# Constant TensorE products around the parameter transposes of a two-block transformer kernel

## The chip, the cores and the metric

One NeuronCore of a Trainium2 chip runs the whole program. The metric is the time of one execution on the device in microseconds (us), and the median over runs is compared. Times of single instructions below come from one profiled execution of the same program.

## What is computed

The reference runs two blocks over 256 tokens of width 1024 in float32. The first block has two layers, each a mixer and an expert stage:

```
for l in range(DEPTH):                      # DEPTH = 2
    mod = silu(c) @ ada_w[l] + ada_b[l]     # shifts, scales and gates
    xm = rms_norm(x, norm_mix_w[l]) * (1 + sc1) + sh1
    proj = xm @ w_in[l]                     # queries, keys, values, pool, gates
    x = x + g1 * ((sigmoid(ga)*attention + sigmoid(gp)*pool) @ w_out[l])
    xf = rms_norm(x, norm_ffn_w[l]) * (1 + sc2) + sh2
    x = x + g2 * peer_ffn(xf)               # top 16 of 16384 experts, 8 heads
x = rms_norm(x, final_norm_w)
for i in range(4):                          # differential, MoBA, window, differential
    x = x + mixer_i(rms_norm_2(x, attn_norm_g[i]))
    x = x + sqrelu_mlp(rms_norm_2(x, mlp_norm_g[i]))
```

`peer_ffn` gathers, for each token and head, 16 rows of `expert_u` and 16 rows of `expert_v` from HBM. The output is the last norm of x.

## The kernel before, in words

The tokens are two tiles of 128 rows and stay in SBUF (`x_res`). Each engine has its own program, and all waits are semaphores written out by hand. The two layers of the first block are one hardware loop on every engine (`Fori(0, DEPTH)`); the four layers of the second block are unrolled.

A weight unit is 1024 x 512. ScalarE rounds a quarter of it to the float32r type (L1367 in the first block, L1491 in the second), VectorE or GpSimd subtracts to get the rest (L1835, L1691, L2407), and TensorE makes three float32r products for one float32 product (`three`, L770, L771, L772). Each is 128x512 wide. Attention, the out projections (L740), the transposes (L706) and the expert products use plain float32.

At the start of a layer of the first block the order is as follows. SyncE loads five small parameter vectors into `prow` (L547 to L551). TensorE waits for them (`s_par`), transposes `prow` into PSUM bank `psT` 0 (L889) and raises `p_tr`. VectorE waits for `p_tr`, sets the same memory to ones (L1919), copies the transposed parameters to `pcol` (L1920), forms shift and scale (L1893 to L1895), waits for ScalarE's sums of squares (L1305), and takes the row statistics (L1629, L1630). ScalarE takes the square root (L1307), VectorE scales the rows (`xn`, L1635), TensorE transposes them in four groups of four (L706), VectorE and ScalarE make the high and low parts of the transposed rows (L1843, L1373, L1853), and TensorE starts the first in-projection (L770). In layer 0 TensorE reaches this point after the last of four column sums of the modulation matrix (`mix_sum`, L865); in layer 1 after the `go` of `layer_end`, with which SyncE lets all engines pass once it has cleared the semaphores (L643).

A gather end is the end of an expert stage: the last expert rows land in `vbuf`, `ring` and `pr`, TensorE multiplies them (L1059), VectorE adds the result to x (L2219, L2220), and the layer ends. There are two, near 1021 us and 1999 us of the profiled execution. After the second, the last four layers begin: TensorE transposes their parameter rows `rows2` (L1105), waits for `p_col`, then for x to be normed (L1638), transposes two groups of it (L706), and starts the first in-projection when ScalarE (L1491, then L1515) and VectorE (L1691, L1740) have made its parts. SyncE's queue loads the lambda vectors and weights there (L655, L666).

PSUM tile `psS` has two banks of 512 floats. Bank 1 is used later in each layer by gate rows, scores and query products.

Of the kernel before, what the change touches and what calls it, by code (L numbers as in the profile page):

```python
# [35 lines left out]
UC = 512  # L36
# [181 lines left out]
def program(nc, T, out):  # L218
    with ExitStack() as ctx:
# [10 lines left out]
        def cst(name):  # L230
            lo, hi = COFF[name]
            return const[:, lo:hi]

        ident = cst("ident")
# [48 lines left out]
        psS = ctx.enter_context(nc.psum_tensor("psS", [P, 2, 512], F32))  # L283
# [234 lines left out]
        def _(sp):  # L518
# [127 lines left out]

            C = Counts(RING2)
            C.slot[0] = -1
            for i, m in enumerate(MIXERS2):
# [10 lines left out]
                def unit2(src, kc=KC, cols=UC):  # L660
                    slot, _ = C.next_slot()
                    if C.unit > RING2:

                        sp.wait_ge(lo_ready, NPC * (C.unit - RING2))
                    dst = ring[:, slot, :, :].rearrange("p k n -> p (k n)")[:, 0:kc * cols]
                    sp.dma_start(dst.rearrange("p (k n) -> p k n", k=kc), src).then_inc(ld[slot], 16)  # L666

                for n, (lo, cols) in enumerate(units):
                    if i == 0 and n == 0:
                        C.next_slot()  # L670
                        continue
# [28 lines left out]
        def _(pe):  # L700
# [13 lines left out]
            def norm(C):  # L714
                C.norm += 1
                C.xn += 2
                pe.wait_ge(xn_ready, C.xn)
                tr_all(C, xn)
# [150 lines left out]
            def ada_sum(n):  # L869
# [10 lines left out]
                                       start=True, stop=True)  # L880
                mm.then_inc(s_ada, 1)

            pe.wait_ge(s_const, 32)
            for n in range(NMIX):
                mix_sum(n, first=True)
            with pe.Fori(0, DEPTH) as l:
                C = Counts()
                pe.wait_ge(s_par, 80)
                pe.transpose(psT[:, 0, 0:76], prow[0:76, :], ident[0:76, 0:76]).then_inc(p_tr, 1)  # L889
                C.tr = 0  # L890
                norm(C)

# [9 lines left out]
                for n in range(8):  # L902
                    first_linear(C, n, sums_in(n))
                    if n == 4:
                        pe.wait_ge(gate_read, 1)
                        pe.wait_ge(lin_used, 4)
                        for g in range(NPG):
                            for kt in range(NT):
# [3 lines left out]
                                               start=(kt == 0), stop=(kt == NT - 1))  # L912
                        mm.then_inc(pl_mm, 1)
                    if n == 5:
                        pe.wait_ge(pl_cp, 1)
                        pe.wait_ge(s_wide, 80)
                        for g in range(NPG):
                            mm = pe.matmul(psT[:, g // 2, (g % 2) * S:(g % 2 + 1) * S], mixw[:, g, :], mT[:, g, :],
                                           start=True, stop=True)
# [183 lines left out]
            C.slot[0] = -1  # L1103
            pe.wait_ge(s_rows, 96)
            pe.transpose(psT[:, 0, 0:80], rows2[0:80, :], ident[0:80, 0:80]).then_inc(p_tr, 1)  # L1105
            pe.wait_ge(p_col, 1)

            def row_groups(C, first, used=None):
# [174 lines left out]
        def _(act):  # L1283
# [236 lines left out]
            for i, m in enumerate(MIXERS2):  # L1520
                if m is DIFF:
                    act.wait_ge(lam_x, 3 * (i // 3) + 1)
                    act.activation(st[:, 8:10], st[:, 6:8], ACT.Exp).then_inc(lam_x, 1)
                n_in, widths = (4, [2 * cols for _, cols in SWA_UNITS]) if m is SWA else (6, [D] * 6)
                high_with_xT(C, pcol[:, 8 * i:8 * i + 8], w=widths[0])
                row_squares(C)
# [954 lines left out]
```

## Time and profile before

| what | value |
|---|---|
| median of 3 runs | 3300.11 us (3299.2 to 3303.0) |
| span of the profiled execution | 3298.6 us |
| TensorE busy | 2344.9 us (71%) |
| VectorE busy | 2128.5 us (65%) |
| ScalarE busy | 936.9 us (28%) |
| GpSimd busy | 1009.8 us (31%) |
| mean granted TensorE clock | 0.832 |

### The profile page before, as it was taken

What the parts mean: (1) busy time and instruction counts of PE and PEld (TensorE: products, weight loads), DVE (VectorE), ACT (ScalarE), POOL (GpSimd) and SP (SyncE); (2) the same over time, 40 slices, a digit from 0 to 9 for tenths busy, and PEclk for the clock granted to TensorE, in tenths of its full rate; (3) what the DMA queues carried; (4) which work ended last, traced back from release to release, by engine and by line L of the source; (5) the groups of instructions that cost most, each with busy time, mean ns of one, the idle gap of its engine ahead of it and who ended that gap; (6) DMA issues with size and microseconds to landing.
All of it is one profiled execution on the core that took longest, in us unless ns stands there. A gap on an engine that the chain in (4) does not pass through costs nothing.

```text
span 3298.6 us, 35236 instructions
## 1 busy us (share of the span) xinstructions
PE 2344.9 (71%) x12383; PEld 1724.4 (52%) x12383; DVE 2128.5 (65%) x4436; ACT 936.9 (28%) x1486; POOL 1009.8 (31%) x1044
## 2 busy tenths in 40 slices
PE   4997444454336996544444337899999999999898
PEld 3855222222004854222222005699879978987797
DVE  6965876677757865776677755565655555555654
ACT  2411111011003501111111004454555444445443
POOL 0201766767771102766667760000000000000000
PEclk9998667777667997666777668799999987999899
DMA  8764999999998754999999994245525532553353
GB/s 316 280 226 140 406 407 407 408 406 409 405 405 306 268 211 174 407 407 407 407 409 409 400 407 180 77 173 185 182 99 179 182 111 103 185 187 140 103 192 126
DMA packets 311815, 892.92 MB, mean 271 GB/s; under 512 B 22424, under 2 KB 31616, under 8 KB 311552
## 3 DMA queue, kind: packets, MB, share of 16 engines
q0 software_dynamic: 147456, 536.94, 41.0%
q1 hardware_dynamic: 164224, 354.32, 30.1%
q8 instruction: 68, 1.11, 0.1%
q14 instruction: 67, 0.55, 0.0%
HBM read 890.13 MB, written 1.05 MB: 270 GB/s over the span
## 4 chain that ended last, share of the span: by engine, by line
PE 46%; DMA 15%; POOL 13%; issue 13%; DVE 11%; ACT 1%; SPq 0%; DVEq 0%; POOLq 0%; ACTq 0%; PEld 0%
DMA proj<-in_expert_u,eidx 13%; PE lin L770 8%; PE lin L771 8%; PE lin L772 8%; POOL proj L2423 7%; POOL vbuf L2436 3%; PE lin L740 3%; POOL ring L2436 3%; PE psS L821 2%; DVE proj L2130 2%; PE psT L772 2%; PE psT L771 2%; PE psS L771 2%; PE psS L772 2%; PE psT L770 2%
## 5 line engine op out<-in xcount | busy, mean ns | idle before, releaser
L2130 DVE CUSTOM_DVE_ANT_0 proj<-proj,psT 128x1024 f32<-128x1024 f32 x512 | 615.2, 1219 | 360.1 <-DMA proj<-in_expert_u,eidx 339.2
L1691 DVE TENSOR_TENSOR weights_split<-ring,weights_split 128x1024 fp32r<-128x1024 f32 (+1 forms) x376 | 450.5, 1207 | 376.3 <-ACT weights_split L1491 373.8
L2423 POOL DMA_INDIRECT proj<-in_expert_u,eidx x512 | 485.0, 947 | 573.8 <-DVEq L2104 318.0
L1491 ACT ACTIVATE weights_split<-ring 128x1024 fp32r<-128x1024 f32 (+1 forms) x376 | 391.5, 1046 | 467.7 <-PE lin L772 291.6
L1046 PE MATMUL psS<-const,pT 128*128 128x16 f32 x64 | 18.8, 373 | 430.6 <-DVE pT L2117 392.8
L1059 PE MATMUL lin<-ring,rowb 128*32 128x512 f32 x896 | 171.1, 802 | 207.1 <-DMA pr<-in_expert_v,pT 138.2
L770 PE MATMUL lin<-weights_split,xT_high 128*128 128x512 f32 (+1 forms) x736 | 297.2, 404 | 11.3 <-DVE xT_low L1740 5.2
L772 PE MATMUL lin<-weights_split,xT_high 128*128 128x512 f32 (+1 forms) x736 | 288.9, 393 | 0.0
L1059 PE MATMUL lin<-vbuf,rowb 128*32 128x512 f32 x1024 | 183.1, 867 | 130.9 <-DVE rowb L2157 130.9
L1434 ACT ACTIVATE gel<-hdot 128x16 f32<-128x16 f32 x32 | 6.9, 216 | 934.2 <-DVE hdot L2130 934.2
L2436 POOL DMA_INDIRECT vbuf<-in_expert_v,pT x256 | 240.1, 938 | 78.1 <-issue 77.5
L1046 PEld LDWEIGHTS psS<-const,pT 128*128 128x128 f32 x64 | 16.0, 311 | 471.0 <-DVE pT L2142 379.6
L1015 PE MATMUL psS<-xT,ring 128*128 128x256 f32 x1024 | 244.9, 400 | 3.1 <-ACT pT L1415 3.1
L1015 PEld LDWEIGHTS psS<-xT,ring 128*128 128x128 f32 x1024 | 203.4, 202 | 62.6 <-issue 33.5
L2436 POOL DMA_INDIRECT ring<-in_expert_v,pT x224 | 210.2, 938 | 68.3 <-issue 66.5
L770 PE MATMUL lin<-weights_split,act_split 128*128 128x512 f32 x512 | 200.1, 391 | 0.0
L771 PE MATMUL lin<-weights_split,act_split 128*128 128x512 f32 x512 | 199.5, 390 | 0.0
L772 PE MATMUL lin<-weights_split,act_split 128*128 128x512 f32 x512 | 199.2, 389 | 0.0
L1059 PEld LDWEIGHTS lin<-ring,rowb 128*32 128x32 f32 x896 | 32.6, 130 | 306.3 <-DMA pr<-in_expert_v,pT 165.9
L771 PE MATMUL lin<-weights_split,xT_low 128*128 128x512 f32 (+1 forms) x480 | 187.3, 390 | 0.0
L770 PEld LDWEIGHTS lin<-weights_split,xT_high 128*128 128x128 f32 x736 | 143.3, 195 | 46.1 <-issue 10.4
L1059 PEld LDWEIGHTS lin<-vbuf,rowb 128*32 128x32 f32 x1024 | 39.2, 147 | 235.8 <-issue 233.6
(279 smaller groups left out, 5008.2 us busy)
## 6 DMA issues: line engine op xcount, KB each, us to landing
ring<-in_mlp_w_up SPq DMA_DIRECT2D x32, 2048.0 KB, 8.7
ring<-in_mlp_w_down SPq DMA_DIRECT2D x32, 2048.0 KB, 7.7
ring<-in_w_in SPq DMA_DIRECT2D x16, 2048.0 KB, 10.0
ring<-in_w_query SPq DMA_DIRECT2D x16, 2048.0 KB, 18.3
vbuf<-in_ada_w SPq DMA_DIRECT2D x12, 2048.0 KB, 12.0
ring<-in_diff_w_in SPq DMA_DIRECT2D x12, 2048.0 KB, 8.1
ring<-in_ada_w SPq DMA_DIRECT2D x8, 2048.0 KB, 12.5
ring<-in_moba_w_in SPq DMA_DIRECT2D x6, 2048.0 KB, 7.9
```

The lines of the kernel that those rows point to most:

```text
L740: mm = pe.matmul(lin[:, pair + t, :], lhs[:, k, t * P:(t + 1) * P], rhs[:, k, :], start=(k == 0), stop=(k == kc - 1))
L770: pe.matmul(out_ap, lhs[0], rhs[0], start=first, stop=False, skip_group_check=True)
L771: pe.matmul(out_ap, lhs[1], rhs[0], start=False, stop=False, skip_group_check=True)
L772: return pe.matmul(out_ap, lhs[0], rhs[1], start=False, stop=last, skip_group_check=True)
L821: mm = pe.matmul(psS[:, g % 2, t * S:t * S + n], qkT[lo:hi, qb, t * P:(t + 1) * P], qkT[lo:hi, kb, 0:n], start=True, stop=True)
L1015: mm = pe.matmul(psS[:, 1, (b % 2) * S:(b % 2 + 1) * S], ring[:, j, k, b * P:(b + 1) * P], xT[:, k, :], start=(k == 0), stop=(k == KC - 1))
L1059: mm = pe.matmul(lin[32 * b:32 * b + 32, 2 * half + t, :], wst[:, cb % 2, 4 * b + s, :], vrow(SETROWS * s + b)[:, half * 512:(half + 1) * ...
L1491: act.activation(part(p, 0, kind, w), raw_piece(slot, p, kind, w), ACT.Copy).then_inc(hi_ready, 1)
L1691: dve.tensor_tensor(part(p, 1, kind, w), raw_piece(slot, p, kind, w), part(p, 0, kind, w).bitcast(F32), ALU.subtract).then_inc(lo_ready, 1)
L2130: dve.tensor_tensor_reduce(ubuf[:, n % GB, :], ubuf[:, n % GB, :], x_row, 1.0, 0.0, ALU.mult, ALU.add, hdot[:, cb, k:k + 1]).then_inc(h_re ...
L2423: pool.indirect_dma_start(out=ubuf[:, (16 * cb + k) % GB, :], out_offset=None, in_=table["u"], in_offset=bass.IndirectOffsetOnAxis(ap=eidx ...
L2436: pool.indirect_dma_start(out=vrow(SETROWS * s + b), out_offset=None, in_=table["v"], in_offset=bass.IndirectOffsetOnAxis(ap=eidxT[:, cb % ...
```

## The change

In the TensorE program a function `keep_clock(n)` issues n float32 products. The stationary operand is the 128x128 identity, the moving one the first 512 columns of the constant pool table, and the result goes to `psS` bank 1. Nothing reads it, they wait for nothing, and they signal nothing. Both operands are loaded at the program's start (`s_const`, waited for ahead of the loop).

- Ahead of the wait for `s_par` and the transpose L889: 6 products, in layer 0 and in layer 1.
- Behind that transpose: 3 products, in both layers.
- Behind the transpose L1105, ahead of the wait for `p_col`: 7 products, once.

```diff
+            def keep_clock(n):
+
+                for _ in range(n):
+                    pe.matmul(psS[:, 1, :], ident, cst("pool")[:, 0:UC], start=True, stop=True, skip_group_check=True)
+
             pe.wait_ge(s_const, 32)
             for n in range(NMIX):
                 mix_sum(n, first=True)
             with pe.Fori(0, DEPTH) as l:
                 C = Counts()
+                keep_clock(6)
                 pe.wait_ge(s_par, 80)
                 pe.transpose(psT[:, 0, 0:76], prow[0:76, :], ident[0:76, 0:76]).then_inc(p_tr, 1)
+                keep_clock(3)
                 C.tr = 0
                 norm(C)
...
             pe.wait_ge(s_rows, 96)
             pe.transpose(psT[:, 0, 0:80], rows2[0:80, :], ident[0:80, 0:80]).then_inc(p_tr, 1)
+            keep_clock(7)
             pe.wait_ge(p_col, 1)
```

## Rows read from the trace of the kernel before

**Rows 1.** The page: span, busy time of each engine, engines of the chain that ended last.

```profile
span 3298.6 us, 35236 instructions
...
PE 2344.9 (71%) x12383; PEld 1724.4 (52%) x12383; DVE 2128.5 (65%) x4436; ACT 936.9 (28%) x1486; POOL 1009.8 (31%) x1044
...
PE 46%; DMA 15%; POOL 13%; issue 13%; DVE 11%; ACT 1%; SPq 0%; DVEq 0%; POOLq 0%; ACTq 0%; PEld 0%
```

**Rows 2.** The chain that ended last, in time order, layer 0's first half: start, us, what.

```profile
54.58 1.13 PE psT L706 x4
...
59.99 0.76 PE lin L770
...
63.31 0.29 PE lin L771
64.06 0.23 PE lin L771
...
192.86 12.02 PE lin L740 x28
```

**Rows 3.** The timeline around layer 0's parameter transpose.

```profile
47.48 1.87 PE L865 MATMUL psS<-const,rope_t 128*128 128x1 f32 x8 [4.04 <-DVE rope_t L1861]
...
49.21 0.37 PE L889 MATMUL psT<-const,prow 76*128 76x76 f32 x1
...
50.07 0.17 DVE L1919 MEMSET prow<- 128x128 f32 x1 [0.45 <-DVE modc L1913]
...
52.41 0.17 DVE L1629 TENSOR_SCALAR st<-st 128x2 f32<-128x2 f32 x1 [1.28 <-ACT tokb L1305]
```

**Rows 4.** The timeline around layer 1's parameter transpose.

```profile
1019.14 1.08 PE L1059 MATMUL lin<-ring,rowb 128*32 128x512 f32 x3
...
1019.99 1.08 PE L1059 MATMUL lin<-ring,rowb 128*32 128x512 f32 x3
...
1022.54 0.35 SPq L547 DMA_DIRECT2D prow<-in_ada_b  x1
...
1026.65 0.39 PE L889 MATMUL psT<-const,prow 76*128 76x76 f32 x1 [5.56 <-DMA prow<-in_pool_scale]
...
1027.26 0.17 DVE L1919 MEMSET prow<- 128x128 f32 x1 [3.26 <-remote]
...
1028.35 0.17 DVE L1629 TENSOR_SCALAR st<-st 128x2 f32<-128x2 f32 x1
```

**Rows 5.** The timeline at the start of the last four layers.

```profile
1999.91 0.28 PE L1105 MATMUL psT<-const,wrow 80*128 80x80 f32 x1 [0.98 <-SPq L643]
...
2007.15 1.94 PE L706 MATMUL psT<-const,x_res 128*128 128x128 f32 x8 [6.96 <-DVEq L2248]
...
2009.91 1.54 ACT L1515 ACTIVATE xT_high<-psT,pcol 128x256 fp32r<-128x256 f32 x4
...
2012.36 0.79 PE L770 MATMUL lin<-weights_split,xT_high 128*128 128x512 f32 x1 [3.27 <-DVE xT_low L1740]
```

**Rows 6.** TensorE by stretch: us, busy us (instructions), granted clock, DMA share, GB/s.

```profile
1030.00:1036.00 6.00, 4.26 (x17) 0.50 0.95 311
...
1990.00:1990.50 0.50, 0.14 (x4) 1.00 0.08 33
1995.00:1995.50 0.50, 0.07 (x4) 0.76 0.00 0
...
2015.50:2016.00 0.50, 0.50 (x3) 0.76 0.00 0
...
2138.50:2139.00 0.50, 0.50 (x4) 0.88 0.00 0
```

**Rows 7.** The timeline after the first attention of the last four layers.

```profile
2133.92 0.80 PE L770 MATMUL lin<-weights_split,xT_high 128*128 128x512 f32 x1 [0.99 <-DVE xT_low L1740]
```

**Rows 8.** TensorE by stretch again, two attention stretches of the last four layers.

```profile
2094.50:2124.50 30.00, 27.93 (x90) 0.50 0.00 1
...
2410.00:2440.00 30.00, 30.00 (x189) 1.00 0.00 1
```

## The prediction

> **What bounds the kernel now.** I read the page first. The span is 3298.6 us; the median of the runs is 3300.11, so 1.5 us lie around it. TensorE is busy 71% of it, VectorE 65%, and 46% of the chain that ended last is TensorE's [rows 1]. No engine bounds it all: the change must be read at its three places.
>
> The chain in time order shows what counts there. In layer 0 it goes from the last column sum over ScalarE's squares and the norm to TensorE's transposes at 54.58, then over VectorE and ScalarE to the first in-projection at 59.99 [rows 2]. Its products stand 0.43 us apart until 63.3 and 0.23 us from then on: they began at half clock and went to full. At the last four layers it is alike: products begin at 2012.36 and the granted clock changes between 2015.5 and 2016.0 [rows 5, 6]. About 3.4 us, or 8 products, run at half clock, and layer 1 has the same code. Saving that is worth 8 x (0.43 - 0.23) = 1.6 us a place.
>
> The timeline then shows what TensorE could be late for. In layer 0 the parameter transpose follows the column sums with no wait; `prow` has long landed [rows 3]. In layer 1 it waits 5.56 us for it, until 1026.65, and in the last part TensorE idles 6.96 us between its parameter transpose and the next ones [rows 4, 5].
>
> **The price of one product.** The 128x512 float32 products of the out projection take 12.02 us for 28, 0.43 us each at full clock [rows 2]. At half clock the expert products, 128x512 float32 too, start 0.85 us apart (1019.14, 1019.99) [rows 4]. So 6 products cost 5.1 us at half clock; if the clock rises after 3.4 us of them, 4 are slow and 2 fast: 4 x 0.85 + 2 x 0.43 = 4.3 us. The first in-projections rose after 3.3 to 3.4 us [rows 2, 5, 6], so I take 4.3. The upper end is 5.1: after the first attention products began at 2133.92 and the clock rose only between 2138.5 and 2139.0 [rows 6, 7].
>
> **Six ahead, layer 0.** Nothing hides them. TensorE ends its column sums at 49.35 and has the transpose ready to go, so the transpose is 4.3 us late (upper 5.1). VectorE waits for it at L1919, and everything of VectorE's is queued behind. But its statistics at 52.41 had waited 1.28 us for ScalarE [rows 3], and ScalarE's squares wait for nothing that is late. So the layer is 4.3 - 1.3 = 3.0 us late (upper 3.8). SyncE's queue is not delayed; its weights have landed or are on their way, and later loads wait for pieces of VectorE and TensorE that are late too, so nothing takes the delay back. Lower end: 0, if some transfer behind it ends the waits anyway.
>
> **Six ahead, layer 1.** SyncE issues the first load behind the `go` at 1022.54, so TensorE starts its products at about 1022.7 and ends at 1027.0 (upper 1027.8). The load they cover ends its wait at 1026.65 [rows 4]. The transpose is 0.3 us late (upper 1.2), and here VectorE has no slack: it waited for the transpose, and its statistics followed its own work at 1028.35 without a wait [rows 4]. So +0.3.
>
> **Three behind.** 1.3 us at full clock, 2.6 at half. In layer 0 5.0 us lie between the end of the parameter transpose (49.21 + 0.37) and the row transposes at 54.58 [rows 2, 3], 3.7 once its slack of 1.3 is used up; in layer 1 the steps between are the same. They are covered and cost nothing. Without this cover they would cost their 1.3 us.
>
> **Seven ahead of the last four layers.** 3.0 us at full clock, 6.0 at half. `p_tr` is raised ahead of them, so VectorE's copy isn't late; TensorE's wait for `p_col` is met meanwhile. They end at 2003.2 to 2006.2, and the next transposes start at 2007.15 [rows 5]. Cost 0. If x were normed earlier by over 0.9 us, the slow case would begin to cost.
>
> **What the clock gives back.** After the three products TensorE idles 3.7 - 1.3 = 2.4 us to the row transposes. The record has an idle of 3.1 us that the full clock outlived (products again at 1990.4, clock 1.00) and another of 3.1 us that it did not (1995.4, clock 0.76 in that half us) [rows 6]. So at 2.4 us I take full clock for the first transposes. Four of these take 1.13 us from their wake to their end at half clock [rows 2], and half of that is pace: 0.5 us saved a layer, 1.0 in all. Bounds: 0, if the six did not raise the clock, and 0.5.
>
> From there to the first in-projection are 5.4 us (54.58 to 59.99) in which TensorE only transposes and waits for VectorE. At full clock it would be busy for about 2 of them. At half clock the stretch from 1030 to 1036 had it busy 4.26 of 6 us, and the clock did not rise [rows 6]. That sort of work is thin; I take it that the clock falls before or soon after the in-projection begins, and that its 3.4 slow us stay. Bounds: 0 and 1.6 us for each layer. At the last four layers, 4.3 us without any product lie between the transposes (over at about 2008.1) and 2012.36, and those first transposes wait to be read until 2009.91 by ScalarE's own queue [rows 5]. Earlier transposes bring nothing, and the idle is longer than the 3.1 us that ended full clock. I take 0; bounds 0 and 1.6.
>
> The Trainium skill, in "TensorE: Matmul & The Clock Gate", Part 4: PE-mode transpose, says that transposes do not count as TensorE activity in the way of products. The row of 1030 to 1036 agrees so far. By it the in-projections' slow start stays in every case, and the sum is the one below; without it, it would be up to 3.2 us lower, as in the first rival.
>
> **The sum.** 3.0 + 0.3 - 1.0 = +2.3 us against the profiled execution, 3298.6 to 3300.9, and with the 1.5 us around it 3302.4. That is 0.07%. A measurement of this kernel can tell about 0.2% (6.6 us) from no change: so, within it.
>
> **Rivals.**
> - *The clock holds through to the in-projections.* Then 1.6 us go at each of three places: 2.3 - 4.8 = -2.5, 3297.6. For it: an idle of 3.1 us once did no harm, and the transposes may count. Against: the thin 5.4 us, and the 4.3 us of nothing in the last case. Also within 0.2%. Chance 0.12.
> - *The products are just in the way.* The six never raise the clock while they last, as after the first attention, where 4.7 us of work went by first; no transposes are faster; and the in-projections, shifted, also wait 4.7 us for the clock instead of 3.4, 0.6 us more at each of three. 3.8 + 1.2 + 1.8 = +6.8, 3306.9. It decides once the rise comes over 4.3 us after the products begin. This is also how the change would fail to do what it says. For it: one such case among three rises read [rows 6, 7]. Chance 0.14, half of it over 0.2%.
> - *A long stretch changes its clock (slower).* In the last four layers two attentions hold quite different states: 30 us at half clock with TensorE busy 27.93, and 30 us at full clock with it busy all the time [rows 8]. A busy engine thus does not always win its clock back. If the shift of some us made the one at 2410 fall and stay, it would cost 15 to 30 us: 3317 to 3332. It decides if TensorE's work thins out for a moment there. Against: the three runs lie within 3.8 us of each other, so such a flip seems rare. Chance 0.08.
> - *The same, faster.* One of the slow attentions keeps full clock and gives up to 14 of its 28 busy us; I take 10: 3292. Same evidence against. Chance 0.06.
>
> **How the numbers follow.** The forecast has 0.60, for 3302.4. Faster by over 0.2% is the last rival, 0.06, and one in a hundred for luck: 0.07. Slower by over 0.2% is half of the second and the third: 0.15. The rest, 0.78, is no change. The range takes in the first two rivals with their ends, 3297 to 3308; the two clock flips are left out, 0.14.
>
> **What would show it.** In the changed kernel's timeline: in layer 0 six products from 49.35, four of them 0.85 us apart, and the parameter transpose near 53.6; VectorE's statistics 3 us later than 52.41, and no wait for ScalarE ahead of them. In layer 1 the transpose near 1027 us plus layer 0's shift. Row transposes at the pace of full clock in both layers. In the last part seven products 0.43 us apart, over before the transposes. All three first in-projections with about 8 products 0.43 us apart: if they start 0.23 apart, I was wrong about the thin stretch. If the layer starts less late than the transpose minus 1.3 us, the delay found slack that I did not see. A changed clock in an attention stretch would overrule all of it.

## The result and the profile after

| | before | after |
|---|---|---|
| median | 3298.77 us (20 runs, 3286.67 to 3303.04) | 3307.60 us (20 runs, 3290.86 to 3312.26) |
| span of the profiled execution | 3298.6 us | 3305.8 us |

The ratio on record is 1.0033, 95% interval 1.0022 to 1.0045: slower by 0.33%, past the 0.2% that I took for the limit of a measurement. The medians alone lie 8.8 us (0.27%) apart. The median lies inside my range at its upper edge, but the forecast was "no change". The runs of both kernels fall into two groups, which the three runs that I had did not show: 3 of 20 of before lie at 3286.7 to 3287.6 and the other 17 have a median of 3299.8; of after, 3 lie at 3290.9 to 3297.7 and the other 17 have a median of 3309.3. The profiled pair below differs by 7.2 us, a little less than the medians do.

The page after. TensorE is busy 16.4 us more than before and the span is 7.2 us longer [rows 1]:

```profile
span 3305.8 us, 35336 instructions
...
PE 2361.3 (71%) x12433; PEld 1727.3 (52%) x12433; DVE 2128.1 (64%) x4436; ACT 936.6 (28%) x1486; POOL 1006.6 (30%) x1044
...
PE 47%; DMA 15%; POOL 13%; issue 12%; DVE 10%; ACT 1%; SPq 1%; POOLq 0%; DVEq 0%; PEld 0%; ACTq 0%
```

The instructions of the added line (count, shortest, median and longest ns, first and last start, forms), in the changed kernel:

```profile
L886 PE MATMUL psS<-const x50: 592/592/1201, 49.2 to 2013.0; 128*128 128x512 f32 x50
```

The code issues 9 + 9 + 7 = 25 products. The profile counts **50 matmul instructions: a plain float32 product of 128x128x512 is two**. The trace of before had said so too. The same view of its out projection:

```profile
L740 PE MATMUL lin<-ring,xT x256: 592/592/676, 186.6 to 1238.1; 128*128 128x512 f32 x128
...
L740 PE MATMUL lin<-vbuf,xn x64: 592/592/595, 216.8 to 1208.9; 128*128 128x512 f32 x64
```

These are 320 instructions for 160 products in the code (two layers of 4 x 8 x 2 + 2 x 4 x 2). The 0.43 us that I took as the price of a product [rows 2] is that of half a product.

The timeline of the changed kernel in layer 0, which answers to [rows 2, 3] (start, us, what, and in brackets the idle time before and what ended it):

```profile
49.17 7.54 PE L886 MATMUL psS<-const 128*128 128x512 f32 x12
...
56.55 0.23 PE L895 MATMUL psT<-const,prow 76*128 76x76 f32 x1
56.62 2.78 PE L886 MATMUL psS<-const 128*128 128x512 f32 x6
56.88 0.17 DVE L1927 MEMSET prow<- 128x128 f32 x1 [7.28 <-PE psT L895]
...
57.96 0.17 DVE L1637 TENSOR_SCALAR st<-st 128x2 f32<-128x2 f32 x1
...
60.13 1.09 PE L706 MATMUL psT<-const,xn 128*128 128x128 f32 x8 [0.73 <-DVE xn L1643]
...
65.54 0.47 PE L770 MATMUL lin<-weights_split,xT_high 128*128 128x512 f32 x1 [1.56 <-DVE first_xT_low L1861]
65.85 0.40 PE L771 MATMUL lin<-weights_split,first_xT_low 128*128 128x512 f32 x1
66.08 0.40 PE L772 MATMUL lin<-weights_split,xT_high 128*128 128x512 f32 x1
```

The six products take 7.5 us. VectorE waits 7.28 us for the transpose behind them, and no longer waits for ScalarE. The products of the first in-projection now start 0.23 us apart: "warm" in what follows, and "cold" where they start 0.43 us apart, at half clock.

Layer 1 in the changed kernel, which answers to [rows 4]:

```profile
1022.42 0.61 PE L1066 MATMUL lin<-ring,rowb 128*32 128x512 f32 x3
...
1029.00 7.43 PE L886 MATMUL psS<-const 128*128 128x512 f32 x12 [5.97 <-issue]
1036.27 0.23 PE L895 MATMUL psT<-const,prow 76*128 76x76 f32 x1
...
1045.25 0.47 PE L770 MATMUL lin<-weights_split,xT_high 128*128 128x512 f32 x1 [1.56 <-DVE first_xT_low L1861]
1045.56 0.39 PE L771 MATMUL lin<-weights_split,first_xT_low 128*128 128x512 f32 x1
```

SyncE's first load starts at 1025.43. TensorE's products, which wait for nothing, start only 3.57 us behind it; I had them 0.2 us behind it. The transpose comes 10.84 us behind the load, 4.11 before.

The last four layers, which answer to [rows 5]:

```profile
2007.39 6.21 PE L886 MATMUL psS<-const 128*128 128x512 f32 x14
2014.51 1.06 PE L706 MATMUL psT<-const,x_res 128*128 128x128 f32 x8 [0.91 <-DVEq L2256]
2019.72 0.80 PE L770 MATMUL lin<-weights_split,xT_high 128*128 128x512 f32 x1 [4.14 <-DVE xT_low L1748]
2020.31 0.63 PE L771 MATMUL lin<-weights_split,xT_low 128*128 128x512 f32 x1
```

The seven products end 0.9 us ahead of the next transposes: covered, with little to spare. From the parameter transpose to the first in-projection it is 12.45 us in both kernels.

TensorE by stretch in the changed kernel (us, busy us (instructions), granted clock, DMA share, GB/s), which answers to [rows 6]:

```profile
1030.00:1040.00 10.00, 9.27 (x20) 0.84 1.00 346
1040.00:1046.00 6.00, 3.00 (x19) 1.00 1.04 388
...
2019.50:2023.00 3.50, 3.28 (x8) 0.51 0.17 66
```

Where the 7.2 us arise, from starts of the same instructions in both profiled executions (after minus before, cumulative):

| place | us |
|---|---|
| parameter transpose, layer 0 | +7.34 |
| first in-projection | +5.55 |
| first out projection | +4.42 |
| first gather of expert rows | +3.44 |
| SyncE's first load of layer 1 | +2.89 |
| parameter transpose, layer 1 | +9.62 |
| first in-projection | +9.32 |
| first out projection | +8.03 |
| first gather of expert rows | +7.03 |
| parameter transpose, last layers | +7.36 |
| end | +7.21 |

### The profile page after: what moved, and what is told of

Read it like the earlier page. It is cut to its first block, busy times and chain, and to the rows that moved or that the text cites. A ratio compares the mean times of both kernels' runs of the same rounds, so it can differ in the third digit from the quotient of the medians.

```text
span 3305.8 us, 35336 instructions
## 1 busy us (share of the span) xinstructions
PE 2361.3 (71%) x12433; PEld 1727.3 (52%) x12433; DVE 2128.1 (64%) x4436; ACT 936.6 (28%) x1486; POOL 1006.6 (30%) x1044
## 4 chain that ended last, share of the span: by engine, by line
PE 47%; DMA 15%; POOL 13%; issue 12%; DVE 10%; ACT 1%; SPq 1%; POOLq 0%; DVEq 0%; PEld 0%; ACTq 0%
DMA proj<-in_expert_u,eidx 13%; PE lin L770 8%; PE lin L771 8%; PE lin L772 8%; POOL proj L2431 7%; POOL vbuf L2444 4%; PE lin L740 3%; POOL ring L2444 3%; PE psS L821 2%; PE psT L772 2%; PE psT L771 2%; PE psS L771 2%; PE psS L772 2%; PE psT L770 2%; PE psS L770 2%
## 5 line engine op out<-in xcount | busy, mean ns | idle before, releaser
L1499 ACT ACTIVATE weights_split<-ring 128x1024 fp32r<-128x1024 f32 (+1 forms) x376 | 391.5, 1046 | 467.7 <-PE lin L772 291.5
L1022 PE MATMUL psS<-xT,ring 128*128 128x256 f32 x1024 | 246.1, 401 | 3.1 <-ACT pT L1423 3.1
L770 PEld LDWEIGHTS lin<-weights_split,xT_high 128*128 128x128 f32 x736 | 142.7, 194 | 49.4 <-issue 11.5
## 6 DMA issues: line engine op xcount, KB each, us to landing
vbuf<-in_ada_w SPq DMA_DIRECT2D x12, 2048.0 KB, 11.9
```

The lines of the kernel that those rows point to most:

```text
L770: pe.matmul(out_ap, lhs[0], rhs[0], start=first, stop=False, skip_group_check=True)
L1022: mm = pe.matmul(psS[:, 1, (b % 2) * S:(b % 2 + 1) * S], ring[:, j, k, b * P:(b + 1) * P], xT[:, k, :], start=(k == 0), stop=(k == KC - 1))
L1499: act.activation(part(p, 0, kind, w), raw_piece(slot, p, kind, w), ACT.Copy).then_inc(hi_ready, 1)
```

## The experiments

In runs 1 to 4 the gathers take as long as in the first profile. In runs 5 to 14 each of the two gathers takes 57 to 72 us longer, and the kernel before, run beside them, is over 110 us slower too; there its totals spread over some 35 us, so I compare each run with before beside it, and mechanisms by stretches between starts. The record numbers the chip 6 for runs 1 to 4 and again for 13 and 14, 3 for runs 5 to 8 and 5 for 9 to 12: whether the chip makes the difference is not shown. "Attention" below is that of the last four layers. The three sites are called six, three and seven. In the expectations, the relu is ScalarE's first activation behind an attention.

**1. Only the three behind the transpose.**

```diff
                 pe.transpose(psT[:, 0, 0:76], prow[0:76, :], ident[0:76, 0:76]).then_inc(p_tr, 1)
+                keep_clock(3)
```

> Only the three products behind the parameter transposes stay. Theory A (a float32 product of 128x128x512 is two matmul instructions, and the six ahead of the transpose are the whole loss): in layer 0 the three run as six instructions from 49.6 to 54.0 or 54.7, against row transposes at 54.58 before, so they cost 0 to 0.2 us; the clock rises during them, the first in-projection starts 0.23 us apart, and layer 0 and layer 1 each gain 1 to 2 us: 2 to 4 us faster than before. Rival B (only the long run of all nine raises the clock, three cannot): parameter transposes on time, first in-projection at 0.43 us a product as before, 0 to +0.5 us.

3299.05 us against 3299.85, ratio 1.0002 (0.9987 to 1.0016). The timeline of this kernel:

```profile
49.05 4.39 PE L886 MATMUL psS<-const 128*128 128x512 f32 x6
54.26 1.10 PE L706 MATMUL psT<-const,xn 128*128 128x128 f32 x8 [0.81 <-DVE xn L1641]
...
59.66 0.77 PE L770 MATMUL lin<-weights_split,xT_high 128*128 128x512 f32 x1 [1.55 <-DVE first_xT_low L1859]
60.23 0.63 PE L771 MATMUL lin<-weights_split,first_xT_low 128*128 128x512 f32 x1
60.65 0.63 PE L772 MATMUL lin<-weights_split,xT_high 128*128 128x512 f32 x1
```

Three products, six instructions, take 4.39 us, nearly what I had forecast for six products, and the row transposes are not late: covered. But the in-projections start 0.43 us apart again. These products run in cover and buy nothing.

**2. Only the six ahead.**

```diff
+                keep_clock(6)
                 pe.wait_ge(s_par, 80)
```

> Only the six ahead of the parameter transposes stay. Theory A: twelve instructions, parameter transpose 7.3 us late in layer 0 (5.5 us late on VectorE) and some 6.5 us more in layer 1. Without the three behind, TensorE idles 3.5 us ahead of the row transposes, the clock falls, and less is given back: +8 to +12 us. Rival B (the three behind do nothing): the same as the whole change, +7 us, with the in-projections at full clock from their start.

3311.16 us, ratio 1.0045 (1.0028 to 1.0062); the profiled span is 11.5 us longer than before's. The whole loss comes with the six. It is larger than the change's 7.2 us: in layer 0 the in-projection began cold here, and the first gather came 7.5 us late, where the change had 3.4.

**3. Only the seven ahead of the last layers.**

```diff
             pe.transpose(psT[:, 0, 0:80], rows2[0:80, :], ident[0:80, 0:80]).then_inc(p_tr, 1)
+            keep_clock(7)
```

> Only the seven ahead of the last four layers stay. Theory A: they fill an idle of TensorE, over before 2007.15, and the first in-projection starts at 2012.36 at half clock as before: 0 us, within 1. Rival B (they help the last layers, or harm them by what runs beside them): a change of over 1 us between the parameter transpose of the last layers and the end.

3289.68 us, ratio 0.9989 (0.9971 to 1.0007). The stretch where the products are is the same to 0.01 us (12.45). The low median comes from elsewhere: 7 of the 12 runs lie below 3292, in the lower of the groups told of above, and in the profiled one the stretch that holds the last attention takes 320.4 us against 328.1 before. Runs 1, 4, 5, 8 and 13, without the seven, have the same quick stretch, so the seven are not needed for it (of the 32 executions of before beside this run, 8 lie below 3292). Effect of the seven: none found.

**4. One product ahead instead of six, alone.**

```diff
+                keep_clock(1)
                 pe.wait_ge(s_par, 80)
```

> One product ahead of the parameter transposes, no others. Theory A (behind the jump back of the layer loop TensorE has no instructions for some 3.5 us, so that what stands ahead of the transpose in layer 1 cannot use the wait for the parameters): in layer 1 its two instructions start 3.5 us behind SyncE's first load of the layer and end after the parameters have landed, the transpose is 1.2 us late there and 1.7 us late in layer 0 (0.4 on VectorE): +1.6 us. Rival B (TensorE is ready at the release and something about the six delays them): the product starts 0.2 us behind SyncE's first load and is over long before the parameters land; layer 1 is not late: +0.4 us.

3299.37 us, ratio 1.0006 (0.9991 to 1.0021). Layer 1 in this kernel's timeline:

```profile
1020.00 0.35 SPq L547 DMA_DIRECT2D prow<-in_ada_b  x1
...
1023.55 2.05 PE L886 MATMUL psS<-const 128*128 128x512 f32 x2 [5.95 <-issue]
...
1025.39 0.34 PE L895 MATMUL psT<-const,prow 76*128 76x76 f32 x1
```

One product also starts 3.55 us behind the load. So the late start doesn't depend on their number. In before no product showed it: there the first thing that TensorE does is the transpose, 4.11 us behind the load.

**5. The six in layer 0 alone.**

```diff
+            keep_clock(6)
             with pe.Fori(0, DEPTH) as l:
```

> The six products stand ahead of the layer loop, so that layer 0 alone has them; nothing else is added. Theory A (twelve instructions on the path in each layer): the parameter transpose of layer 0 at about 56.6 and the first in-projection 5.5 to 6 us late as with the six in both layers, layer 1 as before; +3 to +5.5 us at the end, under half of the six in both layers. Rival B (layer 1 bears it all, since layer 0 has slack behind): back at 0 to +1 us by the end of layer 0.

3430.88 us against 3428.7, ratio 1.0005 (0.9979 to 1.0030): total inconclusive. By stretch: the transpose at 56.30 (+7.1), the in-projection +5.3; in layer 1 the transpose is 4.16 us behind the load, as before. Layer 0 has its cost and layer 1 has none: the two layers pay separately.

**6. Three ahead instead of six, the rest as in the change.**

```diff
-                keep_clock(6)
+                keep_clock(3)
```

> The whole change with three products ahead of the parameter transposes in place of six. Theory A (two instructions a product, and in layer 1 a start 3.5 us behind the release): ahead of the transpose 6 instructions, 4.3 to 5.1 us, instead of 12; transpose of layer 0 near 53.9, which is what was forecast for six; in layer 1 the transpose 7.9 to 8.7 us behind SyncE's first load of the layer instead of 4.1 before and 10.8 with six. About 2.6 us less in each layer than the change: +2 to +4 us. Rival B (the loss hangs on the rise of the clock and not on the count): all six instructions slow, the in-projections slow, +6 us or more.

3432.48 us, ratio 1.0006 (0.9983 to 1.0029), inconclusive as a total. Its timeline in layer 0:

```profile
49.00 4.27 PE L886 MATMUL psS<-const 128*128 128x512 f32 x6
53.11 0.23 PE L895 MATMUL psT<-const,prow 76*128 76x76 f32 x1
```

The transpose comes 4.1 us behind the first product, at 53.11: the 4.3 us and the 53.6 of my forecast, for half the products. The in-projection is +2.1 us (forecast: 4.3 - 1.3 - 0.5 = 2.5), and in layer 1 the transpose is 9.05 us behind the load. One, three and six products (runs 4, 6 and the change) put the transpose 1.85, 4.11 and 7.38 us behind their first start: the price rises nearly in step with their number, and six cost 7.4 us where I had 4.3.

**12. The whole change again**, on chip 5.

> The changed kernel again, beside the others. Theory A: layer 0's parameter transpose at 56.5, layer 1's 10.8 us behind SyncE's first load of the layer (4.1 before), some 7 to 9 us over the kernel before when runs of the same attention state are compared, whatever state this profile has. Rival B (the changed kernel is slow because its shift puts the attentions in the slow state): in the fast attention state it is within 3 us of the fast group before.

3429.42 us against 3412.67, ratio 1.0055 (1.0037 to 1.0073). The timeline:

```profile
1090.96 0.35 SPq L547 DMA_DIRECT2D prow<-in_ada_b  x1
...
1094.53 7.07 PE L886 MATMUL psS<-const 128*128 128x512 f32 x12 [5.96 <-issue]
...
1101.43 0.23 PE L895 MATMUL psT<-const,prow 76*128 76x76 f32 x1
```

Start 3.57 us behind the load, transpose 10.47: the same picture, and the loss repeats.

**13. Where the 3.5 us go: six products ahead of the wait for `go`, three behind the transpose.** The seven are left out. TensorE has already reported that it has arrived.

```diff
-                layer_end(pe, l)
+                pe.sem_inc(arrive, 1)
+                keep_clock(6)
+                wait_loop(pe, go, l + 1)
```

> The six products of layer 1 stand at the end of the layer loop instead, behind TensorE's arrival and ahead of its wait for the release; the three behind the parameter transposes stay. Theory A (the 3.5 us without an instruction belong to the jump back of the loop, wherever the products are): the products start within 0.5 us of the last expert product, since nothing is jumped over, run 5.1 to 10.2 us as twelve instructions, and then comes a pause of about 3.5 us ahead of the parameter transpose with no work in it, though the parameters have long landed; the transpose 8 to 10 us behind SyncE's first load. Rival B (the pause belongs to the release by semaphore, or to the products themselves): a pause ahead of the products, or none at all, and the transpose follows them within 0.5 us.

A single execution, 3412.61 us, beside a median of 3414.0 of before. The timeline:

```profile
1087.28 0.61 PE L1065 MATMUL lin<-ring,rowb 128*32 128x512 f32 x3
...
1087.82 5.42 PE L886 MATMUL psS<-const 128*128 128x512 f32 x12
...
1090.28 0.35 SPq L547 DMA_DIRECT2D prow<-in_ada_b  x1
...
1093.85 0.26 PE L894 MATMUL psT<-const,prow 76*128 76x76 f32 x1 [0.62 <-DMA prow<-in_pool_scale]
...
1102.94 0.47 PE L770 MATMUL lin<-weights_split,xT_high 128*128 128x512 f32 x1 [1.57 <-DVE first_xT_low L1861]
1103.25 0.40 PE L771 MATMUL lin<-weights_split,first_xT_low 128*128 128x512 f32 x1
```

I had expected a pause behind the products (8 to 10 us from the load to the transpose) and missed: there is none. The products follow the last expert product at once, the release comes while they run (until 1093.2), and the transpose starts 3.57 us behind the load. So the 3.5 us belong to the way from the release back to the loop's top, not to products, and products put ahead of it cost layer 1 nothing. They even pay there: the in-projection starts warm, 9.1 us behind the transpose (9.3 before), and the gather comes 260.5 us behind the load, where before has 263.5. This is one profile, and its total can't show 3 us; behind the loop's last pass the same six products also run ahead of the last layers.

**7 and 9. Products inside attention instead.** In the attentions of the last four layers TensorE has work nearly without a gap and yet half clock [rows 8]. One narrow product for each head of the two differential attentions:

```diff
+                if m is DIFF:
+                    keep_clock(1, lin[:, g % 2, 256:512], 256)
```

> The kernel before, and in the two differential attentions one product of 128x128x256 ahead of each head's value products, 16 in all. Theory A (the run times fall in two groups 12 us apart because the last differential attention keeps or loses the full clock, with TensorE just too thinly busy to hold it): both attentions hold the full clock, 8 us each and no group at 3300 any more: 3278 to 3288. Rival B (such products are in the way like those of the change; 16 of 0.43 to 0.85 us on a busy TensorE): the clock falls as before, +5 to +12 us.

> The kernel with one 128x128x256 product ahead of each head's value products in the two differential attentions, again. Theory A (the two groups of run times are the two clock states of these attentions, and the fill makes the fast one certain): no run near 3300, all within 3283 to 3292, and the two attentions some 89 to 91 us from their first scores to the first relu instead of 97. Rival B (the fast state seen in its first profile was luck, as in other profiles): two groups of times remain, the slower near 3300 to 3310.

Totals 3428.64 us (0.9991, 0.9970 to 1.0012) and 3412.1 us (1.0004, 0.9983 to 1.0025): no gain shows. One of run 7's 12 executions took 7652.45 us, the others 3417.55 to 3435.51; what it was is not known. The stretches do differ. The first attention takes 90.4 and 90.3 us against 97.0 in the profile of before, from its scores to the first activation behind it, the last attention's stretch 320.9 in both against 328.1 (from the first such activation of the third layer to that of the fourth). Together that is 13.9 us, while run 9's interval leaves no room for a gain over 5.8. Attentions are as quick in some kernels without these products (both are in runs 5 and 13), so before beside run 9 may often have been quick itself; no profile of it is on record.

**8. Products between the row transposes** (three behind the parameter transpose; then 256, 256 and 512 columns behind the second, third and fourth group).

```diff
+                    if k:
+                        keep_clock(1, cols=(0, 0, 256, 0, 256, 0, UC)[k])
```

> Three products behind the parameter transposes as in the change, none ahead and no seven; and behind the second, third and fourth group of row transposes one product each, 256, 256 and 512 wide, where TensorE waits for VectorE. Theory A (the clock falls in the thin stretch between the row transposes and the in-projection): both first in-projections start at 0.23 us apart, 1 to 1.6 us gained in each layer: -1.5 to -3 us. Rival B (these fillers delay the transposes behind them by more than the clock gives back): 0 to +1.5 us.

3425.15 us, ratio 0.9990 (0.9968 to 1.0012). Here the in-projections start warm and on time; the timeline of layer 0:

```profile
58.03 1.02 PE L704 MATMUL psS<-const 128*128 128x512 f32 x2
59.76 0.47 PE L776 MATMUL lin<-weights_split,xT_high 128*128 128x512 f32 x1 [0.71 <-DVE first_xT_low L1866]
60.07 0.40 PE L777 MATMUL lin<-weights_split,first_xT_low 128*128 128x512 f32 x1
```

From the in-projection to the first gather layer 0 takes 250.5 us, 249.9 in before. The warm start of this layer bought nothing that reaches the gather. In layer 1 it did: warm as well, 247.8 us for the same stretch, 250.1 in before.

**10 and 14. Products in the window attention too.**

```diff
+                if m is DIFF or m is SWA:
+                    keep_clock(1, lin[:, g % 2, 256:512], 256)
```

> The same fill in the window attention of the third layer too, which ran at half clock for 41 to 44 us in every profile. Theory A: it holds the full clock there, 16 products cost 6.9 us and the clock gives back 12 to 18: a further 5 to 10 us, 3275 to 3285. Rival B (that attention is bound by others, or the fill is too thin): the clock falls all the same and the 16 products cost 7 to 14 us there.

> The fill of the differential and window attentions once more, to have its gain on another chip and beside more runs. Theory A (the gain is TensorE's clock in the third layer, 10 to 13 us, and the slow state of the last attention never comes): 8 to 12 us below the kernel before, no slow group. Rival B (the gain of the run before was the chip's gathers): within 3 us of it.

3401.72 us, ratio 0.9971 (0.9956 to 0.9986), and again 3404.0 us, ratio 0.9965 (0.9943 to 0.9987). **This beats both kernels** (run 12, the change on the same chip as run 10, has 3429.42). TensorE by stretch in the window attention, first before, then this kernel:

```profile
2712.00:2742.00 30.00, 30.00 (x114) 0.50 0.00 1
```

```profile
2820.00:2850.00 30.00, 28.93 (x187) 1.00 0.00 1
```

At half clock TensorE completes 114 instructions in 30 us with no gap; at full clock 187. From the first activation behind the second attention to that behind the window attention it takes 290.1 us against 303.1 in the profile of before, and against 300.0 in the kernels whose last attention is quick by itself (runs 1, 3 and 4 among them).

**11. Runs 8 and 10 together**: the edits of both.

> The fill of all three attentions, and in the first block's layers three products behind the parameter transposes with fills behind the row transpose groups. Theory A: 1 to 3 us below the run with the attentions alone, since the first in-projections start at full clock and nothing is ahead of the transposes. Rival B (what a warm start gives is lost again at the next rise): within 1 us of it.

3400.57 us, ratio 0.9966 (0.9950 to 0.9983), 1.2 us from run 10: run 8's products add nothing that can be told.

## Why the prediction was right and wrong

**The price of one product failed.** I took 4.3 us for the six products in layer 0; they took 7.3 us, since each is two instructions, and I divided the time of a row that counts instructions. By my own working with 12 of them, 4 x 0.85 + 8 x 0.43 = 6.8 us, near the 7.34 measured; my 3.4 us to the rise was 4.3 (the first six start 0.82 to 1.00 us apart, until 53.5). Run 6 shows it from the other side. This term was +3.0 us short in layer 0 and as much in layer 1. The rival "just in the way" came within 1 us of the result (3306.9), but by another way, so that is luck: the clock did rise, and the in-projections of both layers did start warm.

**The start in layer 1 failed.** I started the products at 1022.7, 0.2 us behind the load, as the transpose L1105 [rows 5] starts 0.2 us behind SyncE's next load, where no jump lies between. Runs 4, 12 and the change have 3.55 to 3.57 us, runs 2 and 6 3.8. The added delay is thus 3.57 + 7.27 - 4.11 = 6.73 us, where I had 0.3: 3.4 us from the start, 3 from the price. The wait for `prow` covered at most 0.5 us of products, not 4: in every kernel its first instruction behind the release comes 3.55 us or more behind the load. Run 13 excludes the products themselves as the cause. The trace shows what goes with it: packets on queues that it calls instruction. The DMA view of the changed kernel from 1024 to 1030 has, in queue 8 (packets, MB, share):

```profile
q8 instruction: 1, 0.02, 1.0%
```

In all 16 profiled executions such a packet of 16 KB starts 1.1 to 1.7 us behind SyncE's first load of layer 1, and TensorE's first instruction behind the release comes 1.5 to 1.7 us behind that packet's end, whether that is 3.55 us behind the load or 4.43. In before the packet ended 2.5 us behind the load, so by my estimate TensorE was ready at about 4.0, hardly ahead of the transpose at 4.11. Around the transpose L1105, where there is no jump, no instruction packet lies within 4 us. So fetching the loop's code anew after the jump is the likely cause; that queue 8 is TensorE's is not on record, and no run took the jump away.

**Right: what lies beside the path.** The slack of 1.3 us in layer 0: the delay of 7.34 became 5.55 (1.28 of slack, 0.5 of faster transposes, both as worked out; in layer 1 the transposes gave 0.3). The three at nothing (run 1) and the seven at nothing (run 3), though both are twice as long as I thought: the seven took 6.2 us of a cover of 7.1, and by my bound of half clock throughout they would have taken 11.9. That was luck.

**Wrong: the thin stretch.** I took it that the clock falls among the transposes, and put the in-projections' gain at nothing. In the changed kernel it held in both layers: from 1040 to 1046 TensorE was busy 3.00 of 6 us, with transposes until 1043.7 and the first products from 1045.25, at a clock of 1.00, and the in-projections began 0.23 us apart. Run 1 has the same transposes behind three products only, and there it fell. It can even rise among them. Run 3 adds nothing to layer 0; its timeline there:

```profile
54.24 1.97 PE L706 MATMUL psT<-const,xn 128*128 128x128 f32 x8 [4.99 <-DVE xn L1641]
56.45 1.88 PE L706 MATMUL psT<-const,xn 128*128 128x128 f32 x8 [0.24 <-DVE pr L1849]
59.65 0.47 PE L770 MATMUL lin<-weights_split,xT_high 128*128 128x512 f32 x1 [1.32 <-DVE first_xT_low L1859]
59.96 0.40 PE L771 MATMUL lin<-weights_split,first_xT_low 128*128 128x512 f32 x1
```

The first eight transposes take 1.97 us as in before, the second eight 1.88 where before has 2.27, and the in-projection starts warm, with nothing but transposes since 49.0. By the Trainium skill, "TensorE: Matmul & The Clock Gate", Part 4: PE-mode transpose, transposes do not count as activity in the way of products. I let that speak for a slow start in every case; run 3 is against it, and the measurement decides. The last in-projection starts cold, as forecast (0.51 from 2019.5 to 2023).

**What warmth gives back.** From in-projection to first gather the changed kernel is 2.1 us shorter in layer 0 and 2.3 in layer 1; my rival had 1.6 for each. The 16 profiled kernels bear the size out: 249.6 to 251.3 us in the 15 layers that begin cold, 246.1 to 248.7 in 15 of the 17 that begin warm (250.5 in the other two, layer 0 of run 8 and layer 1 of run 11). Whose doing a warm start is, is another matter. Six kernels have nothing added ahead of layer 0's in-projection: before and run 10 begin it cold, runs 3, 7, 9 and 14 warm, with the same instructions. So the profile of before happened to be a cold one, and layer 0's 2.1 us isn't shown to come from the products; against a warm before the change would be some 9.3 us slower (7.2 + 2.1, an estimate), near the 9.5 between the medians of the two larger groups. In layer 1, six of the seven kernels with nothing added there begin cold, and all five with three or more products ahead (the change, runs 2, 6, 12 and 13) warm. There they help, though in run 2 the clock had fallen by the first row transposes and rose again among them. Even as a whole it is 4.4 us against 14 us of added delay less the 1.3 of slack.

**The spread failed.** I argued from three runs within 3.8 us that a flip of an attention's clock was rare. It is common, 3 of the 20 executions of before and 8 of the 32 beside runs 1 to 4, and worth 11 us (from the last layers' first in-projection to the end 1286.3 us in before, 1275.1 in run 3). Without products in attention the last one is quick in 6 of 11 profiled kernels and the first in 2 of 11; with them both are quick in 5 of 5. Before and after have the same stretches there (328.1 and 328.1), so no flip is in the 7.2 us. What makes it flip from one run to the next stays open.

## What to carry over

Work out the price of an operation from its count in the code, not from the count in the row: one product in the code can be two instructions. Products put in to keep the clock pay where TensorE itself is the bound and stays at half speed with its time full, and cost their own length where another engine waits behind them; so look first for the stretch with busy time near 100% at 0.50. Look at several profiles before you credit a warm start to your edit: the same instructions began layer 0's in-projection at half clock in two profiles and at full clock in four. A wait that covers TensorE in the trace may hide a part that TensorE isn't able to use, such as the way back to a loop's top.

## What the hardware did that I had not expected

- TensorE issues nothing for 3.55 to 3.83 us behind SyncE's first load of layer 1, that is, behind the release and the jump to the top of its hardware loop (the five kernels with products there); without a jump it is 0.2 us. A 16 KB packet on an instruction queue ends 1.5 to 1.7 us ahead of its first instruction each time.
- The clock rose from half to full in run 3 while TensorE did nothing but transposes for over 10 us (from 49.0 to 59.65), by their pace: eight took 1.97 us as in before, the next eight 1.88 against 2.27.
- TensorE at half clock with no gap did not win the full clock back in 30 us of attention, and with one unread product of 256 columns per head it kept it there in runs 10, 11 and 14. The last differential attention, in before:

```profile
3040.00:3060.00 20.00, 20.00 (x63) 0.50 0.00 0
```

The same attention in run 3, with the same instructions and by chance at full clock:

```profile
3030.00:3050.00 20.00, 17.66 (x95) 1.00 0.00 1
```

- The same two gathers took 57 to 72 us longer each in runs 5 to 14 than in the others; whether that is the chip stays open, since the record has the number 6 on both sides.
